# First expert pass's token rows through table products on TensorE instead of an indirect gather, with three experts at fixed places

## The reference, cut to what matters

```python
def moe(h, router_w, router_b, w_gate, w_up, w_down):
    t = h.reshape(B * L, D)
    scores = jax.nn.sigmoid((t @ router_w).astype(jnp.float32))
    sel = (scores + router_b.astype(jnp.float32)).reshape(-1, N_EXPERT_GROUPS, EXPERTS_PER_GROUP)
    ...
    ids = g_best[:, None] * EXPERTS_PER_GROUP + local
    w = jnp.take_along_axis(scores, ids, axis=1)
    w = w / jnp.sum(w, axis=-1, keepdims=True)
    ...
    hid = jax.nn.silu(jnp.einsum('nd,edf->nef', t, w_gate)) * jnp.einsum('nd,edf->nef', t, w_up)
    y = jnp.einsum('nef,efd->nd', hid * gates[:, :, None], w_down)
```

## Time and profile before

| | |
|---|---|
| median of 3 runs | 1058.95 us (1053.79 to 1059.17) |
| the profiled execution | 1064.55 us |
| its span in the profile | 1062.7 us |
| TensorE busy | 972.3 us, 91% of the span |
| VectorE busy | 406.3 us, 38% |
| mean granted TensorE clock | 0.953 of full speed |
| expert passes of layer 0, first gate/up product | 432.78 us |
| expert passes of layer 1, first gate/up product | 888.98 us |

### The profile page before, as it was taken

One profiled execution on the slowest core, in us unless ns is written; L12 is line 12 of the kernel. 1 busy time (PEld: TensorE's weight loads), 2 busy tenths in 40 slices (PEclk: granted clock), 3 DMA queues, 4 the chain that ended last, 5 costly groups with the idle time before them and its releaser, 6 DMA issues.

```text
span 1062.7 us, 13818 instructions
## 1 busy us (share of the span) xinstructions
PE 972.3 (91%) x5556; PEld 497.9 (47%) x5556; DVE 406.3 (38%) x908; ACT 177.8 (17%) x377; POOL 141.6 (13%) x151
## 2 busy tenths in 40 slices
PE   2799999998789996799999789999999976999997
PEld 1555445566564554443443244444555554434432
DVE  0211340114753556552333460350226474532236
ACT  4211100014661010111111151000120101111100
POOL 4100140002760000100000400010000001000003
PEclk9899999999999997699999989999999986999999
DMA  9979658975515001999999722320070008999977
GB/s 335 378 278 338 223 187 281 362 252 160 165 42 218 30 20 40 374 385 392 422 406 387 281 104 66 122 79 1 0 249 40 21 20 348 397 411 421 422 297 297
DMA packets 86693, 245.79 MB, mean 231 GB/s; under 512 B 7408, under 2 KB 22416, under 8 KB 74208
## 3 DMA queue, kind: packets, MB, share of 16 engines
q1 hardware_dynamic: 57952, 199.05, 48.7%
q0 software_dynamic: 8816, 29.04, 7.3%
q10 hardware_dynamic: 19856, 16.76, 5.1%
HBM read 216.71 MB, written 27.33 MB: 230 GB/s over the span
## 4 chain that ended last, share of the span: by engine, by line
PE 83%; DMA 7%; DVE 5%; issue 2%; ACT 2%; POOL 1%; SPq 0%; DVEq 0%; ACTq 0%; POOLq 0%
PE bank L1747 25%; PE bank L1863 17%; PE bank L1759 14%; PE bank L1877 8%; DMA ring<-in_ada_w 4%; PE bank L1703 4%; PE bank L1717 4%; PE bank L1854 3%; PE bank L2046 1%; PE bank L1773 1%; PE bank L2121 1%; DVE x_res L1238 1%; DMA uv<-h_rows,small 1%; PE bank L2038 1%; PE bank L2173 1%
## 5 line engine op out<-in xcount | busy, mean ns | idle before, releaser
L1747 PE MATMUL bank<-ring,h_feat 128*128 128x512 f32 x640 | 282.1, 598 | 3.7 <-issue 2.7
L1747 PEld LDWEIGHTS bank<-ring,h_feat 128*128 128x128 f32 x640 | 120.6, 191 | 151.3 <-issue 150.1
L1863 PE MATMUL bank<-ring,uv 128*32 128x512 f32 (+2 forms) x608 | 164.1, 609 | 1.4 <-ACT uv L969 1.4
L1759 PE MATMUL bank<-ring,h_feat 128*128 128x512 f32 x320 | 148.6, 615 | 0.0
L1863 PEld LDWEIGHTS bank<-ring,uv 128*32 128x32 f32 (+2 forms) x608 | 53.3, 136 | 82.6 <-issue 79.0
L1759 PEld LDWEIGHTS bank<-ring,h_feat 128*128 128x128 f32 x320 | 60.4, 196 | 66.6 <-issue 66.5
L1877 PE MATMUL bank<-ring,uv 128*32 128x512 f32 (+2 forms) x304 | 79.7, 595 | 1.0 <-ACT uv L984 0.6
L1467 DVE TENSOR_TENSOR uv<-uv,bank 128x256 f32<-128x256 f32 x25 | 10.5, 421 | 138.7 <-ACT uv L977 138.7
L1717 PE MATMUL bank<-ring,small 128*2 128x128 f32 x1152 | 38.9, 290 | 24.4 <-DMA ring<-in_ada_w 24.4
L859 POOL DMA_INDIRECT uv<-h_rows,small x25 | 23.7, 947 | 209.2 <-PE bank L1854 165.9
L1863 PE MATMUL bank<-h_feat,uv 128*32 128x512 f32 (+2 forms) x208 | 49.4, 594 | 0.0
(11 more groups left out here) (231 smaller groups left out, 1051.2 us busy)
## 6 DMA issues: line engine op xcount, KB each, us to landing
ring<-in_ada_w SPq DMA_DIRECT2D x16, 2048.0 KB, 14.0
ring<-in_moe_w_gate SPq DMA_DIRECT2D x20, 1024.0 KB, 12.9
ring<-in_moe_w_up SPq DMA_DIRECT2D x20, 1024.0 KB, 15.5
ring<-in_moe_w_down SPq DMA_DIRECT2D x20, 1024.0 KB, 15.3
h_tok<-in_moe_w_down SPq DMA_DIRECT2D x12, 1024.0 KB, 16.6
y_rows<-uv SPq DMA_DIRECT2D x23, 512.0 KB, 14.1
ring<-in_na_w_in SPq DMA_DIRECT2D x4, 2048.0 KB, 16.8
bz<-in_ada_w SPq DMA_DIRECT2D x4, 2048.0 KB, 12.9
```

What stands on the lines that cost most here:

```text
L1747: last = mm(jbank(key)[:, :], HT[:, cc, P * t:P * (t + 1)], w[:, cc, :], start=cc == 0, stop=cc == DC - 1)
L1759: last = mm(jbank(key)[:, :], HT[:, cc, P * t:P * (t + 1)], blk_ap(("out", layer, b))[:, cc, :], start=cc == 0, stop=cc == DC - 1)
L1863: last = mm(bank[2][32 * q:32 * (q + n), :], XT[:, b, cc, 32 * q:32 * (q + n)], w[:, :, cc, :], start=cc == 0, stop=cc == DC - 1)
```

## The change

- Experts 0, 1 and 2 have places 0, 1 and 2 always (`FIXED = 3`), and only the other 13 are ranked. `QUARTERS` and `RANK_AT` are new; the sums stay 52 and 48. Pass 0 is still expert 0 alone; pass 1 is now experts 1 and 2, whose weights SP loads before it waits for the ranking.
- Pass 0 has no gather any more. In `place`, VectorE makes for each tile a 0/1 table of 128 tokens by 128 places of expert 0 (`first_oh`). Behind the index products of the last tile, TensorE multiplies the five tables (as the stationary side) with the h2 rows of the five tiles, in two halves of 512 columns, and adds them up in banks 0 and 1. ScalarE and VectorE copy these banks to `XG`, one half each; then pass 0's transposes follow as before.
- The ranking (`rank_experts`) moves behind this copy in VectorE's program, and the copy of pass 0's transposed rows stands inside it. All token lists are first copied out of the bank (`idx_sb`).
- The small products for pass 1's token list stand in the middle of pass 0's gate/up products (after 2 of 8 chunks). Those of all later passes stand behind pass 0's gate/up products, so the gather of pass 2 is issued with them.

The core of the diff:

```diff
-QUARTERS = [[4, 5, 4, 3, 3, 2, 3, 5, 3, 2, 2, 6, 3, 3, 2, 2], [4, 4, 3, 3, 2, 4, 3, 3, 2, 4, 3, 3, 2, 4, 2, 2]]
-RANK_AT = [[1, 3, 4, 5, 10, 6, 2, 7, 11, 12, 0, 8, 9, 13, 14], [0, 4, 5, 10, 1, 6, 7, 11, 2, 8, 9, 12, 3, 13, 14]]
+FIXED = 3
+QUARTERS = [[4, 3, 3, 2, 6, 2, 5, 3, 3, 3, 2, 4, 5, 3, 2, 2], [4, 3, 3, 2, 4, 3, 3, 2, 4, 4, 3, 3, 2, 4, 2, 2]]
+RANK_AT = [[8, 0, 9, 1, 4, 5, 6, 10, 3, 2, 7, 11, 12], [8, 0, 4, 5, 9, 1, 2, 6, 7, 10, 3, 11, 12]]
-RANKED = E - 1
+RANKED = E - FIXED
...
+                for p in range(1, FIXED):
+                    load_gate_up(layer, p, p)
+                    load_down(layer, p, p)
                 sp.wait_ge(ids_ready, 2 * layer + 1)
-                for p in range(1, WSLOTS):
+                for p in range(FIXED, WSLOTS):
...
-                pool.wait_ge(idx_ready, 3 * layer + 1)
                 pool.wait_ge(h2_stored, 16 * TT * (layer + 1))
...
-                for e in range(passes):
-                    if e in (1, 3):
-                        pool.wait_ge(idx_ready, 3 * layer + (2 if e == 1 else 3))
+                for e in range(1, passes):
+                    if e <= 2:
+                        pool.wait_ge(idx_ready, 4 * layer + 1 + e)
...
+                act.wait_ge(carry_mm, (TT + 1) * layer + 1)
+                nc.scalar.activation(XG[:, 0, 0:512], bank[0][:, :], ACT.Copy).then_inc(first_in, 1)
                 read_xt(0, 0, NPASS * layer + 1)
...
                     dve.wait_ge(pos_done, (TT + 1) * layer + t + 1)
+                    link(nc.vector.tensor_scalar(first_place, pos[:, t, 0:1], 1.0, both[:, 0:1], ALU.add, ALU.mult))
+                    nc.vector.tensor_scalar(first_oh[:, t, :], iota[:, 0:P], 1.0, first_place, ALU.add, ALU.is_equal)\
+                        .then_inc(first_oh_ready, 1)
...
+            def rank_experts(layer):
+
                 dve.wait_ge(idx_mm, (TT + 2) * layer + TT)
-                nc.vector.tensor_copy(idx_i[:, 0:1], idx_low[:, 0:1]).then_inc(idx_ready, 1)
-
+                nc.vector.tensor_copy(idx_sb, idx_all).then_inc(idx_ready, 1)
+                dve.wait_ge(xt_mm, NPASS * layer + 1)
+                nc.vector.tensor_copy(XT[:, 0, 4:8, :], bank[1][:, :].rearrange("p (c n) -> p c n", c=4))\
+                    .then_inc(xt_dve, 1)
                 tt(rank_oh, bc(rank_of, RANKED), row(ranks, RANKED), ALU.is_equal)
+                pass_indices(layer, 0, 1, 2)
...
                     if e == 0:
-                        pass_indices(layer, 1, 3, NPASS)
+                        pass_indices(layer, 1, 2, NPASS)
...
-                read_xt(0, base + 1)
-                pass_indices(layer, 0, 1, 3)
+                dve.wait_ge(carry_mm, (TT + 1) * layer + 1)
+                nc.vector.tensor_copy(XG[:, 0, 512:1024], bank[1][:, :]).then_inc(first_in, 1)
+                rank_experts(layer)
                 route_weights(layer)
...
+                def first_rows(t):
+                    pe.wait_ge(first_oh_ready, TT * layer + t + 1)
+                    pe.wait_ge(h2_ready, TT * layer + t + 1)
+                    for half in range(2):
+                        last = mm(bank[half][:, :], first_oh[:, t, :], H[:, t, 512 * half:512 * half + 512],
+                                  start=t == 0, stop=t == TT - 1)
+                    return last
...
                 indices(TT - 1)
+                for t in range(TT):
+                    last = first_rows(t)
+                last.then_inc(carry_mm, 1)
...
-            def gate_up(b, tiles, slot):
-                for cc in range(DC):
+            def gate_up(b, tiles, slot, chunks=range(DC)):
+                for cc in chunks:
...
                     gate_up_weights(e)
-                    gate_up(b, plan.tiles[e], turn).then_inc(gu_mm, 1)
                     if e == 0:
-                        pass_indices(layer, 1, range(3, passes))
+                        gate_up(b, plan.tiles[e], turn, range(0, 2))
+                        pass_indices(layer, 0, range(1, 2))
+                    gate_up(b, plan.tiles[e], turn, range(2 if e == 0 else 0, DC)).then_inc(gu_mm, 1)
+                    if e == 0:
+                        pass_indices(layer, 1, range(2, passes))
...
-                pe.wait_ge(gathered[0], arrivals(1, 0, 16))
-
-                wait_read(pe, ("r", layer, TT - 1, 0))
-                wait_read(pe, ("r", layer, TT - 1, 1))
+                pe.wait_ge(first_in, 2 * (layer + 1))
                 xt_transposes(0).then_inc(xt_mm, 1)
-                pass_indices(layer, 0, range(1, 3))
                 expert_steps(layer, body)
```

More of the change, by code:

```diff
@@ L142, in gathers_before @@
     def gathers_before(self, s):
-        return len(range(s, self.before.passes, 3)) if self.before else 0
+        return len(range(s or 3, self.before.passes, 3)) if self.before else 0
     def stores_before(self, s):
@@ L501, in expert_steps @@
                 body(e, e % 3, e // 3, (e - 1) // 3)
-        v_normed, ring_free, last_mm = sem("v_normed"), sem("ring_free"), sem("last_mm")
+        v_normed, ring_free, carry_mm = sem("v_normed"), sem("ring_free"), sem("carry_mm")
+        first_oh_ready, first_in = sem("first_oh_ready"), sem("first_in")
         expert_in = [sem(f"expert_in{s}") for s in range(WSLOTS)]
@@ L872, in _ @@
                 pool.wait_ge(xt_mm, NPASS * layer + passes)
-                pool.wait_ge(late_idx_ready, layer + 1)
+                pool.wait_ge(idx_ready, 4 * (layer + 1))
                 for o in range(MAXOV):
@@ L1350, in out_and_route @@
                 nc.vector.tensor_copy(ids_i, ids).then_inc(ids_ready, 1)
-                tt(by_rank, oh_by_rank, row(idx_low[:, 1:E], RANKED), ALU.mult)
+                dve.wait_ge(idx_ready, 4 * layer + 1)
+                tt(by_rank, oh_by_rank, row(idx_low[:, FIXED:E], RANKED), ALU.mult)
                 red(tok_low, by_rank, ALU.add)
@@ L1375, in route_weights @@
                 nc.vector.memset(start[:, 0:1], 0.0)
-                link(nc.vector.memset(cap[:, 0:1], 32.0 * QUARTERS[layer][0]))
+                for p in range(FIXED):
+                    if p:
+                        nc.vector.memset(start[:, p:p + 1], float(PLANS[layer].first_row[p]))
+                    ins = nc.vector.memset(cap[:, p:p + 1], 32.0 * QUARTERS[layer][p])
+                link(ins)
                 for out, table in ((start, first_row), (cap, room)):
                     tt(by_rank, rank_oh, row(table, RANKED), ALU.mult)
-                    red(out[:, 1:E], by_rank, ALU.add)
+                    red(out[:, FIXED:E], by_rank, ALU.add)
                 tt(excess, cnt, cap, ALU.subtract)
@@ L1422, in row_tables @@
                 dve.wait_ge(late_idx_mm, layer + 1)
-                nc.vector.tensor_copy(idx_i[:, NPASS:NTILE], late_sums[:, NTILE:]).then_inc(late_idx_ready, 1)
-                dve.wait_ge(late_idx_ready, layer + 1)
+                nc.vector.tensor_copy(idx_i[:, NPASS:NTILE], late_sums[:, NTILE:]).then_inc(idx_ready, 1)
+                dve.wait_ge(idx_ready, 4 * (layer + 1))
                 link(nc.vector.tensor_copy(row_w, late_sums[:, 0:NTILE]))
@@ L1519, in add_last @@
             def add_last(layer, t):
-                dve.wait_ge(last_mm, TT * layer + t + 1)
+                dve.wait_ge(carry_mm, (TT + 1) * layer + t + 2)
                 left, right = last_banks[layer][t]
@@ L1832, in out_projection @@
                 indices(TT - 2)
+                for h in range(2):
+                    wait_read(pe, ("o", layer, TT - 1, h))
+                    wait_read(pe, ("r", layer, TT - 1, h))
                 positions(TT - 1)
@@ L1836, in out_projection @@
                 indices(TT - 1)
+                for t in range(TT):
+                    last = first_rows(t)
+                last.then_inc(carry_mm, 1)
             def pass_indices(layer, part, passes):
-                pe.wait_ge(ids_ready, 2 * (layer + 1))
-                pe.wait_ge(idx_ready, 3 * layer + 1 + part)
+                pe.wait_ge(idx_ready, 4 * layer + 1 + part)
+                if part:
+                    pe.wait_ge(ids_ready, 2 * (layer + 1))
                 for e in passes:
@@ L1845, in pass_indices @@
                         if k < 4:
-                            last = mm(out, ident[:, 32 * k:32 * (k + n)], tok_low[:, p - 1:p], start=True, stop=True)
+                            toks = idx_low[:, p:p + 1] if p < FIXED else tok_low[:, p - FIXED:p - FIXED + 1]
+                            last = mm(out, ident[:, 32 * k:32 * (k + n)], toks, start=True, stop=True)
                         else:
                             last = mm(out, ident[0:PLACES - P, 32 * (k - 4):32 * (k - 4 + n)],
-                                      tok_high[0:PLACES - P, p - 1:p], start=True, stop=True)
+                                      tok_high[0:PLACES - P, p - FIXED:p - FIXED + 1], start=True, stop=True)
                 last.then_inc(idx_mm, 1)
@@ L1989, in add_last @@
```

(6 more changed lines are left out.)

16 lines of the change are left out of this document (10 added, 6 removed).

## The result

The changed kernel takes 1067.84 us (median of 5 runs, 1066.61 to 1070.15) against 1059.17 for the kernel before: a ratio of 1.0082, 95% interval [1.0057, 1.0106]. A second set of runs gave 1.0073 [1.0050, 1.0097]. So it is slower by 0.7 to 0.8%, where 1055 and most likely no change were forecast. The profiled execution of the changed kernel took 1070.15 us, 5.6 more than that of before.

What follows compares the result with a forecast made beforehand. TensorE was busy 91%, but at the changed place the store, gather and transpose waits bound it. Layer gains of 1.75 and 2.0 us, together 3.75, gave 1060.8 us profiled, 1055.2 on the median; range 1049 to 1061.

Steps and rivals of the forecast that it cites:

- Added, TensorE: Before pass 0: ten 128x512 products at 0.43 us high clock, 0.86 low, take 7.05 us; bounds 4.3 to 8.6.
- The term for the clock: During the ten products: clock starts low and rises 5.5 us later, the mean of the two rises seen before.
- The last case of the rivals: Ten products at twice the row's price add 7 us a layer: 1069 us; within a group given 0.04.
- handover to pass 0: Between products and pass 0: bank copies 0.69 us, signals 0.1, eight transposes 1.1, the copy behind them 0.8.
- from there to pass 1: Layer 0: VectorE's hid ends at 445.1, copies take 0.95 us, pass 1's products start at 446.05.
- pass 1's products: Both layers: the clock falls again before them, so 8.6 us, -0.5 in layer 0 and +0.55 in layer 1.
- clock down in the handover: Copies before pass 0 idle TensorE, the clock falls, pass 0 takes its old 9.56 and 10.16 us: 1060.7; chance 0.12.
- VectorE late: Between passes 0 and 1: ranking and route weights stand behind pass 0's copy, so layer 0's hid ends 1.9 us later.
- TensorE is not in the way: Between passes 0 and 1: index products 2.2 us, transposes done at 444.8, or 445.7 at the low level, in layer 0.
- Late second gather: Pass 1's gather, forecast at 5.5 us, takes 14.2 instead; pass 1 starts +5.6 and +4.4 us: 1069; chance 0.09.
- At nothing: Moved weight loads and place order cost nothing; if expert 4's cover were gone, one megabyte costs 2.6 us.
- The VectorE additions: Two more operations a tile, 0.45 us; tiles 0 to 2 hidden, tiles 3 and 4 add 0.9 us.

Runs made afterwards that it cites:

- the two left behind: Changed kernel with the products of tiles 0 to 3 ahead of the last tile's positions, tile 4's two behind the index products: 1057.18 us, 0.9981 of the kernel before.
- gather put back, loads late: Changed kernel without the ten products, pass 0 gathered from DRAM again, weights of places 1 and 2 loaded behind the ranking: 1068.85 us, 1.0095 of the kernel before.
- gather put back: Changed kernel without the ten products, pass 0 gathered from DRAM again, fixed places and early weight loads kept: 1078.00 us, 1.0168 of the kernel before.

## Why the prediction was wrong, step by step

**The step that failed is "Added, TensorE".** It priced the ten products by "6.87/16 = 0.43 us at the high level". The 16 in that row counts instructions; the source makes 8 calls there (one for each chunk of the features), and the trace shows two instructions for each of these float32 products (a transpose shows as one: eight calls, x8). The "16 products" in the description of a pass are the same count. So the row says 6.87/8 = 0.86 us a call, and I multiplied a price of an instruction by a number of calls. The group after reads x20 for ten calls. Measured, a call costs 0.84 us by the run with the products twice, 0.9 by the two left behind at the high level and 1.6 mostly at the low. The term for the clock was not at fault: with the 3.3 and 5.5 us at the low level read above, and 1.72 and 0.86 us a call, ten calls come to an estimate of 10.3 and 11.4 us. Ten took 10.32 and 11.47 us in place of 7.05, and in place of a gather path that held TensorE idle for 6.4 and 7.7.

**The rule that I set aside was right.** The Trainium skill, page FP8 and Floating Point Precision, TensorE Precision Notes, says that true FP32 takes four passes through the array; with the 215.7 ns of the Trainium skill's page TensorE: Matmul & The Clock Gate (Wait — 56ns, not 53.3ns?) the estimate was 0.86 us a product. The runs agree with it, and so did the trace before: I wrote that it did not, by the same wrong count. The last case of the rivals named that mechanism with 1069 us and only a part of the last 0.04; the range to 1061 left it out.

The steps in us, the first from the out projection's end, the others from the step before:

| step | forecast | layer 0 | layer 1 |
|---|---|---|---|
| index products end | 15.8 | 15.8 | 15.8 |
| ten products | 7.05 | 10.3 | 11.5 |
| handover to pass 0 | 2.7 | 2.8 | 2.8 |
| pass 0's products | 7.3 | 9.1 | 7.5 |
| from there to pass 1 | 4.5 | 4.8 | 4.8 |
| pass 1's products | 8.6 | 8.8 | 8.5 |

- The error of pass 1's start is 5.5 us in layer 0 and 5.0 in layer 1; the products are 3.3 and 4.4 of it.
- The rival **clock down in the handover** came true in layer 0 of the profiled execution and costs 1.5 of the 1.8 us in pass 0's row. It did not come in layer 1, nor in layer 0 of the second profile of the same kernel. The Trainium skill, TensorE: Matmul & The Clock Gate, Part 4, says that transposes do not count as activity in the usual way; the level fell behind them in one profile and not in the other, so the traces neither confirm nor exclude it.
- **VectorE late:** hid did end behind its own chain and not behind ScalarE, as written (907.23 + 0.18, then L1491). But with the chain moved away the time stayed: TensorE's list products and transposes end as late. The forecast's sentence that TensorE is not in the way did not hold: the list products, priced at 2.2 us, ran until 448.6 in layer 0, 2.9 us behind pass 0.
- **Late second gather:** not in the changed kernel; pass 1's transposes waited for no DMA. It was issued later than forecast, 4.9 and 3.2 us behind pass 0's start (441.51 and 899.47) in place of 1.7, but landed after 4.7 us, some 2 us before those transposes. With the weight loads already under way (gather put back, loads late) it took 9.54 and was waited for.
- **At nothing:** the early loads cost nothing that the chain shows, as said, but the cover was priced wrongly. I wrote 2.6 us for a late megabyte; without the early start TensorE waits some 12 us a layer, since pass 1 wants two experts at once. I also overlooked that the weights of place 6 are now wanted a pass sooner in layer 1 (0.54 us).
- The VectorE additions (0.46 us for tile 4's two operations), both copies and the transposes (1.17 us) were as forecast.

What the products displace was not wrong: the gather path did go. With the same products at the same price in the idle time ahead of them, the change is worth 9 to 12 us.

## What to carry to other kernels

Before a row's mean is used as a price, match its count with the calls of the source, and take the price per call. A gather that TensorE waits for can be replaced by 0/1 products, but they pay where TensorE is idle anyway, here ahead of the last tile's positions and not behind the last index products. Here a transfer on the critical path and weight loads started early did not go together (a store of 9.0 us for 3.0): which of the two a layout allows is better decided first.

## What the runs showed that I had not expected

- A 512 KB row store took 2.98 us with quiet queues and 9.01 beside 6 MB of weights. With the gather kept, the early loads made the last stores 6.0 and 5.2 us longer, together more than the whole change cost.
- An indirect gather of 128 rows took the longer the sooner weight loads were issued behind it: 5.10 and 5.93 us where the first load came 1.60 and 0.83 us later (kernel before), 8.67 and 7.95 at 0.62 and 0.69 (gather put back, loads late), 9.07 and 8.84 at the same moment (gather put back). No run varies this distance alone.
- Of three experts' weights asked for together, the fifth matrix of nine landed 18.90 us after its issue, and pass 1 waited for it.
- The same kernel showed the level falling behind a handover in one profile and not in another; 1.5 us of a layer hang on it.
